# Two transformer blocks on one core: opening by channel halves, two modulation sums moved behind the heads, block two's projection thirds spread over more heads

## Chip, cores and metric

The kernel runs on one core of a Trainium2 chip. The metric is the device time of one execution in microseconds (us), from the first instruction to the last. PE is TensorE, DVE is VectorE, ACT is ScalarE, POOL is GpSimd and SP is SyncE, which issues the loads. PSUM is the accumulator memory of eight banks, SBUF the working memory.

## What is computed

The reference runs two blocks on x (256 tokens x 1024 channels, fp32), one after the other. The part that matters here:

```python
def first_block(x, c, ...):
    mod = c @ w_ada + b_ada                        # 1 x 3072
    shift, scl, gate = jnp.split(mod, 3, axis=-1)
    h = rms_norm(x, g_norm) * (1.0 + scl) + shift
    proj = h @ w_in                                # 256 x 5120
    ...                                            # pooling, 8 heads of attention, two up-projections
    x = x + gate * (merged @ w_out)
    return rms_norm(x, g_final)

def second_block(x, c, ...):
    mod = jax.nn.silu(c) @ w_ada + b_ada           # 1 x 6144
    sh1, sc1, ga1, sh2, sc2, ga2 = jnp.split(mod, 6, axis=-1)
    h = _modulate(_rms_norm(x, g_norm_mix), sh1, sc1)
    proj = h @ w_in
    ...                                            # retention (4 heads) and sparse attention (8 heads)
    x = x + ga1 * (jnp.concatenate([ret_out, nsa_out], -1) @ w_out)
    h = _modulate(_rms_norm(x, g_norm_ffn), sh2, sc2)
    x = x + ga2 * _peer(h, ...)                    # computed densely here, over all 16384 experts
    return _rms_norm(x, g_norm_final)
```

The modulation vectors (shift, scale, gate) are matrix-vector products with large fp32 matrices: `ada1` is that of block one (parts 0 to 5 of 512 columns: 0, 1 shift, 2, 3 scale, 4, 5 gate), `ada2` that of block two (parts 0 to 11).

## The kernel before

**Loads.** The weights of both blocks stream through four slots of 2 MB in SBUF (tile `G`), in the order of the list `STREAM` (l. 63). One entry is a *panel*: 512 output columns for all 1024 input channels, loaded as two halves of 512 channels (1 MB each) by SP (l. 673 to 692). Panel n waits until panel n-4 has been used (`panel_used`, l. 582). Between the panels SP issues x, the constants, the rope tables (`tab`) and the gates.

**The order of everything else** is one list that all engines walk, written out by hand in `steps()` (l. 104): each engine executes its own part of each step, in that order. PSUM banks are handed out from that list: banks 0 to 3 in turn (`turn % 4`, l. 246), 4 and 5 for some fixed uses.

**A projection panel** is computed from two *units* (half a panel each). fp32 operands are split into a rounded "high" and a rest "low"; a unit is three *thirds*, each of 8 matmuls of 128x512: high x high (L1134), high weights x low (L1140), low weights x high (L1146). The weights' high part is made by ACT (`unit_high`, L814), their low part by POOL (L740, four operations of 128x512 per unit). The high part of the activations is made by ACT (L799), the low one by DVE (L1821).

**A modulation sum** (`ada`, `sum_step`, l. 1660 to 1684) is 8 steps on DVE, one for each 128 channels: the first a multiplication (L1677), the rest multiply-add (L1679). The running sum lies either in SBUF (`tab`) or in a PSUM bank (`banks`). PE then adds over the partitions. For one part (the "row" panel) PE makes the product itself instead: `make_row` (L1094), 8 matmuls with one output row, then ACT copies that row and `row_columns` (L1101) turns it into columns. `start_columns` (L1108) adds the partitions of an opening sum; DVE turns the columns into scale and shift (L1776 to 1778, L1788, L1790).

**The opening** computes all four of block one's shift and scale parts (ada1-2, -3 and -1 by DVE, ada1-0 by the row), transposes the normed x (L1072), applies scale and shift while it empties the banks (`turn_out`, L1749 on DVE, L852 on ACT), splits the result, and starts with the products of panel in1-2. `keep_busy` (L1086) issues matmuls whose result nobody reads.

**Block one** goes on with panels in1-2 to in1-9, the last seven of them inside the loop over the 8 attention heads (`heads()`: a step `score` L1295, its softmax on ACT and DVE with L1738 as last, transposition `pT` L1303, product `pv` L1322). Then come `y` (L1932), the units of `poolup` and `attnup`, emptied on DVE (L1948; L1950 with L1952), and `out1`.

**Block two** has its own call of `heads()` for heads 8 to 23, with a table `later` of what PE does after each score: units 35 to 38 whole and units 39, 40 and 41 in thirds, retention (`ret` L1456, `retO` L1466, emptied by L1925), gates (`gate` L2030, over the sums of a head's results), and DVE's pieces of the sums ada2-4 and ada2-5. After the last head come `o`, `mT` (L1072 again) and the output projection (L1161, L1165, L1174). The experts' phase follows; the change does not touch it.

## Time and profile before

| | us |
|---|---|
| median of 3 runs | 1250.8 (1247.75 to 1253.36) |
| profiled execution, its own time | 1252.92 |
| its span in the profile | 1251.1 |
| PE busy | 1198.7 (96%) |
| DVE busy | 902.1 (72%) |
| ACT busy | 619.6 (50%) |
| POOL busy | 552.5 (44%) |
| mean granted clock of PE | 0.986 |

The span is that of one profiled execution; its own time is 1.8 us above the span, and 2.1 us above the median. Timeline rows group neighbouring instructions of one line: start, duration of the group from first start to last end, engine, line, operation, output and inputs, shapes, count, and in brackets the idle time before it with what ended it. In all rows L is a line of the kernel before. PE's fp32 matmuls appear as two records each.

### The profile page before, as it was taken

How to read it: one execution, taken by the hardware profiler on the slowest of the kernel's cores; microseconds unless marked ns; L12 is line 12 of the kernel's file. 1: busy time of each engine (PE TensorE's matmuls, PEld its weight loads, DVE VectorE, ACT ScalarE, POOL GpSimd, SP SyncE). 2: the span in 40 equal slices, each digit the busy share in tenths (PEclk: the TensorE clock that was granted, in tenths of full speed). 3: DMA queues.
4: the chain of work that ended last, by engine and by line, in shares of the span. 5: the costliest groups of instructions: out<-in, count | busy, mean ns of one | idle time of the engine just before them, and what ended most of it. 6: DMA issues, size and time to landing. Idle time of an engine off the chain costs nothing.

```text
span 1251.1 us, 19151 instructions
## 1 busy us (share of the span) xinstructions
PE 1198.7 (96%) x7212; PEld 1049.5 (84%) x7212; DVE 902.1 (72%) x1847; ACT 619.6 (50%) x1079; POOL 552.5 (44%) x323
## 2 busy tenths in 40 slices
PE   4999998999999999999999999999999999999996
PEld 2778877776777899999999999999888888888885
DVE  5678648787667625999768999999556656656666
ACT  1555444454535435444466666555454544545453
POOL 0878759584533005888877777776200000000000
PEclk9999999999988999999999999999999999999998
DMA  9988664353341533656555545555566667666664
GB/s 376 418 337 331 269 269 171 135 208 144 126 152 68 202 135 102 186 183 182 180 165 154 164 156 158 160 155 153 167 223 232 189 220 232 190 190 193 194 193 150
DMA packets 54523, 244.28 MB, mean 195 GB/s; under 512 B 6944, under 2 KB 7328, under 8 KB 42016
## 3 DMA queue, kind: packets, MB, share of 16 engines
q1 hardware_dynamic: 54000, 242.34, 56.6%
q8 instruction: 58, 0.95, 0.3%
q10 hardware_dynamic: 432, 0.72, 0.2%
q14 instruction: 33, 0.27, 0.1%
HBM read 240.94 MB, written 2.10 MB: 194 GB/s over the span
## 4 chain that ended last, share of the span: by engine, by line
PE 88%; DVE 5%; POOL 3%; issue 1%; ACT 1%; DMA 1%; SPq 0%; POOLq 0%; DVEq 0%; ACTq 0%
PE bank L1540 10%; PE bank L1537 10%; PE bank L1536 10%; PE banks L1576 5%; PE bank L1582 5%; PE bank L1576 5%; PE banks L1579 5%; PE banks L1582 5%; PE bank L1579 5%; POOL wq_low_r L740 3%; PE banks L1550 3%; PE banks L1134 2%; PE banks L1140 2%; PE banks L1146 2%; PE bank L1134 2%; PE bank L1140 2%
## 5 line engine op out<-in xcount | busy, mean ns | idle before, releaser
L765 POOL TENSOR_TENSOR split_r<-ring,split_r 128x1024 fp32r<-128x1024 f32 x128 | 307.9, 2406 | 157.3 <-ACT split_r L1000 157.2
L1000 ACT ACTIVATE split_r<-ring 128x1024 fp32r<-128x1024 f32 x256 | 269.2, 1052 | 180.2 <-PE bank L1540 180.2
L1536 PE MATMUL bank<-h_high_r,split_r 128*128 128x256 f32 x1024 | 251.2, 283 | 1.7 <-ACT split_r L1000 1.7
L1537 PE MATMUL bank<-h_low_r,split_r 128*128 128x256 f32 x1024 | 251.1, 283 | 0.0
L2161 DVE TENSOR_TENSOR split_r<-ring,split_r 128x1024 fp32r<-128x1024 f32 x128 | 156.8, 1225 | 65.6 <-ACT split_r L1000 65.6
L1536 PEld LDWEIGHTS bank<-h_high_r,split_r 128*128 128x128 f32 x1024 | 195.8, 191 | 1.9 <-issue 1.9
L1537 PEld LDWEIGHTS bank<-h_low_r,split_r 128*128 128x128 f32 x1024 | 195.9, 191 | 0.0
L769 POOL TENSOR_TENSOR small<-small 128x1 f32<-128x1 f32 x2 | 1.5, 761 | 359.0 <-DVE small L2187 359.0
L740 POOL TENSOR_TENSOR wq_low_r<-G,G_r 128x512 fp32r<-128x512 f32 (+1 forms) x104 | 135.7, 1340 | 49.3 <-ACT G_r L814 49.3
L1540 PE MATMUL bank<-h_high_r,split_r 128*128 128x256 f32 x1024 | 143.7, 283 | 0.2 <-POOL split_r L765 0.2
L1054 ACT ACTIVATE gs_r<-G 128x256 fp32r<-128x256 f32 x128 | 53.5, 418 | 172.5 <-PE bank L1582 172.5
L1540 PEld LDWEIGHTS bank<-h_high_r,split_r 128*128 128x128 f32 x1024 | 132.0, 192 | 0.4 <-POOL split_r L765 0.4
L2109 DVE SCALAR_TENSOR_TENSOR hot_r<-bank,x,w_both_r 128x256 fp32r<-128x256 f32 x256 | 105.5, 472 | 0.0
L2159 DVE TENSOR_TENSOR gs_r<-G,gs_r 128x256 fp32r<-128x256 f32 x128 | 54.3, 424 | 61.8 <-ACT gs_r L1054 61.4
L740 POOL TENSOR_TENSOR wq_low_r<-G,hT_r 128x512 fp32r<-128x512 f32 x48 | 64.4, 1376 | 63.0 <-ACT hT_r L814 63.0
L1576 PE MATMUL banks<-split_r,gs_r 128*128 128x512 f32 x254 | 79.1, 393 | 1.8 <-ACT split_r L1000 1.8
L1582 PE MATMUL bank<-split_r,gs_r 128*128 128x512 f32 x254 | 78.2, 389 | 0.0
L1579 PE MATMUL banks<-split_r,gs_r 128*128 128x512 f32 x254 | 78.2, 389 | 0.0
L1576 PE MATMUL bank<-split_r,gs_r 128*128 128x512 f32 x254 | 78.2, 389 | 0.0
L1579 PE MATMUL bank<-split_r,gs_r 128*128 128x512 f32 x254 | 78.2, 389 | 0.0
L1582 PE MATMUL banks<-split_r,gs_r 128*128 128x512 f32 x254 | 78.2, 389 | 0.0
L814 ACT ACTIVATE G_r<-G 128x2048 fp32r<-128x2048 f32 (+1 forms) x26 | 48.6, 1881 | 21.2 <-DMA G<-in_in 17.9
(455 smaller groups left out, 2247.1 us busy)
## 6 DMA issues: line engine op xcount, KB each, us to landing
ring<-in_down SPq DMA_DIRECT2D x128, 512.0 KB, 3.5
ring<-in_up SPq DMA_DIRECT2D x128, 512.0 KB, 3.5
G<-in_ada SPq DMA_DIRECT2D x32, 1024.0 KB, 10.1
G<-in_in SPq DMA_DIRECT2D x32, 1024.0 KB, 7.2
G<-in_out SPq DMA_DIRECT2D x8, 1024.0 KB, 8.1
G<-in_wq SPq DMA_DIRECT2D x8, 1024.0 KB, 7.7
tab<-in_ada SPq DMA_DIRECT2D x4, 1024.0 KB, 5.8
G<-in_poolup SPq DMA_DIRECT2D x2, 1024.0 KB, 6.3
```

Source lines behind the costliest of these rows:

```text
L740: pool.tensor_tensor(low[:, c, :], raw_half[:, c, :], high[:, c, :].bitcast(F32), ALU.subtract)\
L765: pool.tensor_tensor(wsplit[:, j % SPLIT, 1, :], raw[:, j % RAW, :], wsplit[:, j % SPLIT, 0, :].bitcast(F32), ALU.subtract).then_inc(low_r ...
L1000: nc.scalar.activation(wsplit[:, n % SPLIT, 0, :], raw[:, n % RAW, :], ACT.Copy).then_inc(high_ready, 1)
L1536: mm(o, w[0][:, c, :], h_high[:, c, :], start=(c == 0), stop=False)
L1537: mm(o, w[0][:, c, :], h_low[:, c, :], start=False, stop=False)
L1540: ins = mm(o, w[1][:, c, :], h_high[:, c, :], start=False, stop=(c == C - 1))
L1576: mm(o, g[0][:, tok], w[:, 0, cols], start=(n == 0), stop=False, skip_group_check=True)
L1579: mm(o, g[1][:, tok], w[:, 0, cols], start=False, stop=False, skip_group_check=True)
L1582: ins = mm(o, g[0][:, tok], w[:, 1, cols], start=False, stop=False, skip_group_check=True)
L2109: ins = stt(out=O2[m % 2][:, t, :, :], in0=iota_p.unsqueeze(1).to_broadcast([P, 2, P]), scalar=picks[:, 1, tok:tok + 1], in1=w_both[:, :, ...
L2159: tt(gs[n % 2][1], Gv[:, n, :], gs[n % 2][0].bitcast(F32), ALU.subtract).then_inc(gs_low, 1)
L2161: tt(wsplit[:, n % SPLIT, 1, :], raw[:, n % RAW, :], wsplit[:, n % SPLIT, 0, :].bitcast(F32), ALU.subtract)\
```

## The change

**Opening.** The order of the load queue is now written out (`LOADS`), and the opening works by halves of the channels. The first half's scale (ada1-2) and shift (ada1-0, now a DVE sum) come first; the row panel is now ada1-3 (the second half's scale); ada1-1 (the second half's shift) is loaded after the first halves of in1-2 and in1-3 and summed with its running sum in PSUM. The four keep_busy matmuls of the opening are dropped. PE begins the products of both panels' first halves before the second half of the activations exists. From in1-4 on a projection panel is loaded ahead of the modulation panel it is paired with, and each modulation sum stands one panel later; the gates are loaded later, on a semaphore of their own.

**Behind block one's heads.** The sum of ada2-6 (before: inside the heads) and that of ada2-7 (before: 4 + 4 steps behind `y`, running sum in SBUF) now both stand behind `y`, 8 + 8 steps, running sums in PSUM.

**Block two.** Thirds of units 39 to 41 are spread over more heads, three `busy` steps (two unread matmuls each) are put in, the gates stand one head later, and pieces of the sums ada2-4 and ada2-5 move.

```diff
+STREAM += [("ada1", 2, PANEL, "dve"), ("ada1", 0, PANEL, "dve"), ("ada1", 3, PANEL, "row"), ("in1", 2, PANEL, "pe"),
+           ("in1", 3, PANEL, "pe"), ("ada1", 1, PANEL, "dve")]
+for a, b in ((("in1", 4), ("ada1", 4)), (("in1", 5), ("ada1", 5)), (("in1", 0), ("ada2", 2)), ...
+LOADS = [(0, 0), (0, 1), (1, 0), (1, 1), (2, 0), (2, 1), (3, 0), (4, 0), (5, 0), (5, 1), (3, 1), (4, 1)]
+LOADS += [(n, half) for n in range(6, len(STREAM)) for half in range(2)]
...
-    high("in1", 2, (0,))
-    out.extend(("xT", 0, t, half) for t in range(NT) for half in range(2))
-    high("in1", 2, (1,))
-    panel("in1", 2)
+    out.extend([("high", 0), ("xT", 0, 0, 0), ("xT", 0, 1, 0), ("xsplit", 0), ("row",), ("high", 1), ("high", 2), ("high", 3),
+                ("mods",), ("xT", 0, 0, 1), ("xT", 0, 1, 1), ("xsplit", 1), ("proj", "in1", 2, 0), ("proj", "in1", 2, 1)])
...
     out.append(("y",))
-    last = AT["ada2", 7]
-    for n in ada_after(AT[("poolup", None)], ada):
+    last = (AT["ada2", 6], AT["ada2", 7])
+    for n in ada_after(last[0], ada):
         out.append(("ada", n))
-    out.extend(("sum", last, c) for c in range(4))
+    out.extend(("sum", last[0], c) for c in range(C))
     out.append(("high", 23))
     out.extend(("up", "poolup", t, 1) for t in range(NT))
     out.extend(("oT", t) for t in range(NT))
-    out.extend(("sum", last, c) for c in range(4, C))
+    ...
+    out.extend(("sum", last[1], c) for c in range(C))
...
-        [("high", 41), ("third", 39, 0), ("ret", 0), ("ret", 1), ("third", 39, 1), ("third", 39, 2), ("high", 42)] + both(2),
-        [("retO", 0), ("retO", 1), ("ret", 2), ("ret", 3)] + piece(0, 5, 7),
-        [("retO", 2), ("retO", 3), ("retC",), ("high", 43), ("gate_load",)] + piece(0, 7, 8),
-        [("third", 40, 0), ("third", 40, 1), ("gn",)],
-        [("third", 40, 2), ("rn", 0), ("rn", 1)],
-        [("third", 41, 0), ("third", 41, 1), ("ada", gate[0])] + piece(1, 0, 2),
+        [("high", 41), ("third", 39, 0), ("ret", 0), ("ret", 1), ("third", 39, 1), ("high", 42)] + piece(0, 7, 8),
+        [("third", 39, 2)] + both(2),
+        [("retO", 0), ("retO", 1), ("ret", 2), ("ret", 3), ("busy", 0)],
+        [("retO", 2), ("retO", 3), ("retC",), ("high", 43), ("gate_load",)],
+        [("gn",), ("third", 40, 1), ("third", 40, 2)],
+        [("rn", 0), ("rn", 1), ("third", 41, 0)],
+        [("third", 41, 1), ("ada", gate[0])] + piece(1, 0, 2),
         [("third", 41, 2)] + piece(1, 2, 4),
-        [("gate", 0)] + piece(1, 4, 5),
-        [("gate", 1), ("mT", 1, 0, 0)] + piece(1, 5, 6),
-        [("mT", 1, 1, 0), ("wout_head", 0), ("high", 44)] + piece(1, 6, 8)],
+        [("gate", 0)],
+        [("gate", 1), ("mT", 1, 0, 0)],
+        [("mT", 1, 1, 0), ("wout_head", 0), ("high", 44)]],
...
-         8: [("cmpT", 0), ("cmpT", 1)], 9: [("cmpO", 0), ("cmpO", 1)], 12: both(3)}, 2)
+         8: [("cmpT", 0), ("cmpT", 1)], 9: [("cmpO", 0), ("cmpO", 1), ("third", 40, 0)], 13: both(3),
+         14: [("busy", 1)], 15: [("busy", 2)]}, 2)
+    out.extend(piece(1, 4, 8))
...
-                part = ps[4 + k % 2][:, :] if START <= k < BLOCK_ONE else a
+                part = ps[7][:, :] if k == START - 1 else ps[4 + k % 2][:, :] if START <= k < BLOCK_ONE else a
```

On PE in the opening, from its first row. Before (L1108 `start_columns`, L1072 transposes, L1094 the row, L1134/L1140/L1146 a unit's thirds):

```order
L1108 MATMUL banks<-keep,tab 128x1 x4
L1072 MATMUL bank<-keep,G 128x128 x8
L1072 MATMUL banks<-keep,G 128x128 x8
L1108 MATMUL banks<-keep,tab 128x1 x4
L1094 MATMUL bank<-G,small 1x512 x8
L1086 MATMUL bank<-keep 128x384
L1101 MATMUL bank<-keep,G 128x1 x4
L1108 MATMUL bank<-keep,tab 128x1 x4
L1086 MATMUL banks<-keep 128x384 x3
L1134 MATMUL bank<-hT_0_r,ring_r 128x512 x8
```

Now (the same operations, at lines 1119, 1083, 1104, 1112 and 1143 to 1155 of the changed kernel):

```order
L1119 MATMUL banks<-keep,tab 128x1 x4
L1083 MATMUL bank<-keep,G 128x128 x8
L1083 MATMUL banks<-keep,G 128x128 x8
L1104 MATMUL bank<-G,small 1x512 x4
L1119 MATMUL banks<-keep,tab 128x1 x4
L1104 MATMUL bank<-G,small 1x512 x4
L1143 MATMUL banks<-hT_0_r,ring_r 128x512 x8
L1149 MATMUL banks<-hT_0_r,G_r 128x512 x8
L1155 MATMUL banks<-wq_low_r,ring_r 128x512 x8
L1112 MATMUL bank<-keep,G 128x1 x4
L1119 MATMUL bank<-keep,tab 128x1 x4
L1143 MATMUL bank<-G_r,ring_r 128x512 x8
```

The first unit's three thirds now stand ahead of the row's columns and of the third `start_columns`.

On DVE behind block one's heads, from `y` to the emptying of attnup. Before:

```order
L1932 TENSOR_TENSOR G<-bank,G 128x512 x2
L1706 TENSOR_TENSOR small<-bank,small 128x4
L1677 TENSOR_SCALAR tab<-G,small 128x512
L1679 SCALAR_TENSOR_TENSOR tab<-G,small,tab 128x512 x3
L1948 SCALAR_TENSOR_TENSOR G<-G,bank 128x512
L1948 SCALAR_TENSOR_TENSOR G<-G,banks 128x512
L1992 TENSOR_TENSOR G_r<-banks,ring_r 128x4x128
L1992 TENSOR_TENSOR G_r<-bank,ring_r 128x4x128
L1679 SCALAR_TENSOR_TENSOR tab<-G,small,tab 128x512 x4
L1950 SCALAR_TENSOR_TENSOR G<-G,bank 128x512
```

Now:

```order
L1968 TENSOR_TENSOR G<-bank,G 128x512 x2
L1737 TENSOR_TENSOR small<-bank,small 128x4
L1740 TENSOR_SCALAR small<-small 128x4
L1741 TENSOR_TENSOR small<-small 128x4
L1703 TENSOR_SCALAR banks<-G,small 128x512
L1705 SCALAR_TENSOR_TENSOR banks<-G,small,banks 128x512 x6
L1705 SCALAR_TENSOR_TENSOR tab<-G,small,banks 128x512
L1984 SCALAR_TENSOR_TENSOR G<-G,banks 128x512 x2
L2028 TENSOR_TENSOR G_r<-bank,ring_r 128x4x128 x2
L1734 TENSOR_TENSOR small<-banks,small 128x4
L1703 TENSOR_SCALAR banks<-G,small 128x512
L1705 SCALAR_TENSOR_TENSOR banks<-G,small,banks 128x512 x6
```

Two whole sums stand there in place of one, and their running sum is in `banks` (PSUM), not in `tab` (SBUF).

On PE in block two, from score 22 on (L1295/L1296 score, L1072 `mT`, L1303 pT, L1322 to L1324 pv, L1161 the output projection). Before:

```order
L1295 MATMUL banks<-G 128x128
L1296 MATMUL banks<-G 128x256
L1072 MATMUL banks<-keep,ring 128x128 x4
L1303 MATMUL bank<-keep,rows 128x128 x3
L1322 MATMUL bank<-G,ring 128x64
L1323 MATMUL bank<-G,ring 128x64
L1324 MATMUL bank<-G,ring 128x64
L1295 MATMUL bank<-G 128x128
L1296 MATMUL bank<-G 128x256
L1072 MATMUL banks<-keep,ring 128x128 x4
L1161 MATMUL banks<-G_r,ring_r 128x512 x4
```

Now (L1321/L1322 score, L1329 pT, L1348 to L1350 pv, L1097 a busy step, L1083 `mT`):

```order
L1321 MATMUL bank<-G 128x128
L1322 MATMUL bank<-G 128x256
L1329 MATMUL banks<-keep,rows 128x128 x3
L1348 MATMUL bank<-G,ring 128x64
L1349 MATMUL bank<-G,ring 128x64
L1350 MATMUL bank<-G,ring 128x64
L1097 MATMUL banks<-keep 128x384 x2
L1321 MATMUL bank<-G 128x128
L1322 MATMUL bank<-G 128x256
L1083 MATMUL bank<-keep,ring 128x128 x4
L1329 MATMUL banks<-keep,ring 128x128 x3
```

The first `mT` (which needs gate 0) now stands behind score 23, where it stood behind score 22, and a busy step stands ahead of score 23.

## Rows read from the trace of the kernel before

**Rows 1.** The page: busy times, granted clock in 40 slices, the chain that ended last

```profile
PE 1198.7 (96%) x7212; PEld 1049.5 (84%) x7212; DVE 902.1 (72%) x1847; ACT 619.6 (50%) x1079; POOL 552.5 (44%) x323
...
PEclk9999999999988999999999999999999999999998
...
PE 88%; DVE 5%; POOL 3%; issue 1%; ACT 1%; DMA 1%; SPq 0%; POOLq 0%; DVEq 0%; ACTq 0%
```

**Rows 2.** PE's waits over the whole span: total us, times, longest us

```profile
PE banks L1108 <- DMA small<-in_cb: 13.3, 1, 13.3
...
PE banks L1072 <- DVE ring L2030: 2.7, 2, 1.7
...
PE bank L1134 <- DVE G L1948: 1.8, 1, 1.8
...
PE banks L1295 <- DVE ring L1925: 1.3, 1, 1.3
```

**Rows 3.** PE's timeline, 0 to 75 us: start us, us, then the group

```profile
21.94 8.72 PE L1094 MATMUL bank<-G,small 128*1 128x512 f32 x16
...
36.56 2.06 PE L1134 MATMUL bank<-hT_r,ring_r 128*128 128x512 f32 x8 [1.05 <-DVE G L1749]
...
58.94 1.39 PE L1134 MATMUL bank<-G_r,ring_r 128*128 128x512 f32 x5 [0.17 <-issue]
...
69.94 1.02 PE L1205 MATMUL banks<-tab,keep 128*128 128x512 f32 x2
...
71.80 1.12 PE L1072 MATMUL bank<-keep,G 128*128 128x128 f32 x8 [0.40 <-ACT G L878]
...
73.38 0.63 PE L1072 MATMUL banks<-keep,G 128*128 128x128 f32 x4 [0.47 <-DVE rows L1700]
...
74.79 0.46 PE L1295 MATMUL banks<-G 64*128 64x128 f32 x2 [0.78 <-ACT G L901]
```

**Rows 4.** DVE's timeline, 0 to 80 us

```profile
14.91 0.49 DVE L1677 TENSOR_SCALAR tab<-G,small 128x512 f32<-128x512 f32 x1 [2.56 <-DMA G<-in_ada]
15.43 5.47 DVE L1679 SCALAR_TENSOR_TENSOR tab<-G,small,tab 128x512 f32<-128x512 f32 x7
...
24.96 0.48 DVE L1677 TENSOR_SCALAR tab<-G,small 128x512 f32<-128x512 f32 x1 [2.27 <-DMA G<-in_ada]
...
50.06 0.76 DVE L1677 TENSOR_SCALAR banks<-G,small 128x512 f32<-128x512 f32 x1
50.85 4.71 DVE L1679 SCALAR_TENSOR_TENSOR banks<-G,small,banks 128x512 f32<-128x512 f32 x6
```

**Rows 5.** ACT's timeline, 0 to 80 us

```profile
31.30 1.89 ACT L814 ACTIVATE hT_r<-G 128x2048 fp32r<-128x2048 f32 x1
...
33.83 1.51 ACT L852 ACTIVATE G<-banks,small 128x128 f32<-128x128 f32 x4 [0.64 <-DVEq L1791]
```

**Rows 6.** POOL's timeline, 0 to 80 us

```profile
33.27 5.96 POOL L740 TENSOR_TENSOR wq_low_r<-G,hT_r 128x512 fp32r<-128x512 f32 x4 [18.62 <-ACT hT_r L814]
```

**Rows 7.** DVE's timeline, 185 to 196 us

```profile
188.07 1.29 DVE L1932 TENSOR_TENSOR G<-bank,G 128x512 f32<-128x512 f32 x2 [1.17 <-PE bank L1324]
...
190.55 5.06 DVE L1679 SCALAR_TENSOR_TENSOR tab<-G,small,tab 128x512 f32<-128x512 f32 x3
```

**Rows 8.** Windows: stretch, busy us of each engine, PEclk, DMA share, GB/s

```profile
349.00:361.00 12.00, 12.00 (x46) 9.61 (x45) 8.89 (x36) 5.33 (x14) 2.00 (x2) 0.57 0.60 201
383.00:391.00 8.00, 6.98 (x26) 5.46 (x25) 7.40 (x21) 3.64 (x12) 0.00 (x0) 0.57 0.06 26
```

**Rows 9.** PE's timeline, 354 to 421 us

```profile
354.34 3.78 PE L1134 MATMUL banks<-hT_r,ring_r 128*128 128x512 f32 x8
...
364.39 2.12 PE L1146 MATMUL banks<-wq_low_r,ring_r 128*128 128x512 f32 x8
...
417.22 4.03 PE L1086 MATMUL bank<-keep 128*128 128x384 f32 x12
```

**Rows 10.** SP's queue: its timeline, 130 to 215 us

```profile
173.10 22.12 SPq L679 DMA_DIRECT2D G<-in_out  x4
```

More of the change, by code:

```diff
@@ L844, in _ @@
                     ins.then_inc(ready, 1)
+                elif kind == "row":
+                    act.wait_ge(row_full, 1)
+                    nc.scalar.activation(row, ps[6][0:1, :], ACT.Copy).then_inc(row_copied, 1)
+                elif kind == "xsplit":
+                    for q in range(NT):
+                        x0_high_part(q, s[1])
                 elif kind == "xT" and s[2] == 1:
@@ L855, in _ @@
                     bank_free(ins, s)
-                    for q in range(NT):
-                        x0_high_part(q, half)
                 elif kind == "high":
@@ L1113, in _ @@
             start_columns(0)
-            opening = [s for s in STEPS if s[0:2] == ("xT", 0)]
-            for _, _, t, half in opening:
-                if half == 0:
+            opening = [s for s in STEPS if s[0:2] == ("xT", 0) or s[0:2] == ("proj", "in1") and s[2] in (2, 3)]
+            for half in range(2):
+                for t in range(NT):
                     pe_.wait_ge(xn_ready, t + 1)
-                transposes(("xT", 0, t, half), [xn[0][:, t, (4 * half + c) * P:(4 * half + c + 1) * P] for c in range(4)])
+                    transposes(("xT", 0, t, half), [xn[0][:, t, (4 * half + c) * P:(4 * half + c + 1) * P] for c in range(4)])
+            make_row(0)
             start_columns(1)
-            make_row()
-            keep_busy(ps[7], 1)
-            row_columns()
-            start_columns(2)
-            keep_busy(ps[4], 3)
+            make_row(1)
             def products(k, outs, x_high, x_low, chunk, x_ready, thirds=(0, 1, 2)):
@@ L1191, in m_ready, with in1_products, x_ready @@
                 return wait
+            def in1_products(i, halves, fill):
+                steps_ = [("proj", "in1", i, t) for t in range(NT)]
+                outs = [(bank_to_fill(pe_, step) if fill else ps[USE[step][0]], slice(t * P, (t + 1) * P), step)
+                        for t, step in enumerate(steps_)]
+                for half in halves:
+                    def x_ready(low):
+                        pe_.wait_ge(x0_low_ready if low else x0_high_ready, 1 + half if low else 2 + 2 * half)
+                    products(UNIT[AT["in1", i], half], [(o[:, :], tok, step) for o, tok, step in outs],
+                             x0_high, x0_low, 4 * half, x_ready)
+            in1_products(2, (0,), True)
+            row_columns()
+            start_columns(2)
+            in1_products(3, (0,), True)
+            in1_products(2, (1,), False)
+            in1_products(3, (1,), False)
             for s in STEPS:
@@ L1209, in _ @@
                     bank_full(ins, s)
+                elif kind == "busy":
+                    bank = bank_to_fill(pe_, s)
+                    keep_busy(bank, 1).then_inc(full[USE[s][0]], 1)
+                    keep_busy(bank, 1).then_inc(freed[USE[s][0]], 1)
                 elif kind == "warm":
@@ L1697, in ada_out @@
                     g = gateA if name == "ada1" else gate2
+                    if name == "ada1" and half == 0:
+                        dve.wait_ge(gates_in, 48)
                     if name == "ada2" and half == 0:
```

139 lines of the change are left out of this document (71 added, 68 removed).

## Prediction

> **What bounds the kernel now.** I read the page first: PE is busy for 1198.7 of 1251.1 us, and the chain that ended last is 88% PE [rows 1]. So a microsecond is won only where PE stands still, runs slowly, or has matmuls taken away. Next the granted clock by slices: 9 nearly everywhere, with two 8s in the slices from 344 to 407 us and one in the last slice [rows 1]. Then PE's waits, longest first [rows 2]: 13.3 us at the start for the first constants, and behind it only waits of 1 to 3 us. Last the timelines of the two places that the change touches: the opening, where real products start at 36.56 us [rows 3], and block two's heads, where PE has light work and runs at 1.2 instead of 2.4 GHz in two stretches [rows 8]. The experts' phase, two thirds of the span, is not touched.
>
> A measurement of this kernel can tell about 0.5% from no change, 6.25 us of 1250.8.
>
> **The opening.** The load queue sets its pace. The sum of ada1-3 starts at 14.91 and that of ada1-1 at 24.96, each when its first half lands, four halves apart [rows 4]: 2.51 us a half. In the new order, counted from ada1-0's first half at 14.9 (the same place in the queue): ada1-3 at 19.9 and 22.4, in1-2's first half at 25.0, in1-3's at 27.5, ada1-1 at 30.0 and 32.5, the two second halves at 35.0 and 37.5, then the tables and in1-4.
>
> The first product needs unit 0's weights and half 0's activations. ACT rounds the weights in 1.89 us [rows 5], 25.0 to 26.9. It then empties half 0's banks, 1.51 us [rows 5], and rounds the result group by group behind that; I put the activations at 29.4. The shift is in time: ada1-0's sum takes 0.49 + 5.47 us [rows 4] and ends at 20.9. PE meanwhile makes the row, 8.72 us in all [rows 3]: the first half from 19.9 to 24.3, start_columns, the second half until about 29. The first product starts at **29.7** instead of 36.56.
>
> From there four units take 22.4 us, as in the rows (36.56 to 58.94 [rows 3]). Between the first and the second now stand the row's columns and the third start_columns, 1.9 us together. The latter waits for the sum of ada1-1, which starts at about 31.1, when DVE has split half 0, and takes 0.76 + 4.71 + 0.8 = 6.3 us in PSUM [rows 4]: 37.4. PE is there at 36.2, a **new wait of 1.2**. 29.7 + 22.4 + 1.9 + 1.2 = 55.2: in1-4 starts 3.7 us before its 58.94.
>
> Between in1-4 (11.0 us, until 69.94) and score 0 stand three waits of 0.40, 0.47 and 0.78 us [rows 3]. The second is on the gate row of ada1-4, whose product moves a panel later; the other two are on ACT's copies of in1-4, which now start with fewer roundings ahead of them. I take 1.4 of the 1.65. The moved product (1.02 us [rows 3]) comes back inside the heads and counts as no gain. The four keep_busy matmuls that go stood under a wait for DVE: nothing. The opening: **-5.1**. If DVE's sum were no wait at all it would be -6.3; if half of the head start were eaten by landings and splits, -1.7.
>
> The sum's price rests on where its running sum lies. While POOL works, a step takes 1.69 us with it in SBUF (5.06 us for 3 [rows 7]) and 0.785 in PSUM (4.71 for 6 [rows 4]). The Trainium skill, "SBUF — State Buffer", section "SBUF: two separate sides", gives a rule for this: a DVE operation with two SBUF inputs and a GpSimd operation lock one port pair against each other. By that rule, the trace agrees. A rule against the change stands in "VectorE: DVE Perf Modes" of the Trainium skill, section "Why PSUM operands drop a tier": an operand in PSUM rules out the mode that uses both read ports. Here the first step takes 0.76 us in PSUM against 0.49 in SBUF, the next ones 0.785 against 5.47 / 7 = 0.78 [rows 4]. If all eight steps of the two moved sums paid this 0.27, each sum would lose 2.2 us instead of 0.27, and the total below would be 3.8 smaller; by the rows only the first step pays, and that is inside the 6.3.
>
> **Behind block one's heads** PE waits for DVE (1.8 us at L1134 [rows 2]). From `y` (188.07 [rows 7]) on, DVE had one sum in SBUF, 0.8 + 7 x 1.69 = 12.6 us; it now has two in PSUM, 2 x 6.3 = 12.6. Three more small operations come with the sums: **+0.5**. That ada2-6's sum leaves the heads gains nothing, since DVE has slack there. Its slot comes free later, about 196 instead of 170. SP's queue shows out1's loads issued over 22.12 us from 173.10 [rows 10]; the first of them now waits until 196. Load, rounding and POOL's four operations (5.96 at most [rows 6]) take about 13 us more: 209, where PE comes to that unit no earlier than 209 to 214. Hidden, with little to spare.
>
> **Block two.** Removed: the wait of 1.3 us for L1925 and the two for L2030, 2.7 [rows 2], because a third, busy matmuls or another head now stand ahead. The window 349 to 361 has a granted clock of 0.57, so 12 x 0.43 = 5.2 us are lost in it; 383 to 391 likewise 8 x 0.43 = 3.4 [rows 8]. At half clock a third takes 3.78 us instead of 2.12 [rows 9]. Before the first fall PE had some 10 us of the heads' and retention's small matmuls with a wait among them; one third (39, 2) and one busy step now stand there. Before the second it had the waits for the gates; a third and two busy steps now stand there. I take both as mended. Added: three busy steps of two matmuls. Twelve records, six matmuls, take 4.03 us [rows 9], so six cost **+4.0**. New waits: the gates and `o` follow closer behind norm and DVE's moved pieces. No row shows them; between none and twice those that they replace (5.4) I take 2.7, the size of the two at L2030. Sum: -1.3 - 2.7 - 5.2 - 3.4 + 4.0 + 2.7 = **-5.9**.
>
> **Together** -5.1 + 0.5 - 5.9 = -10.5. The profiled execution, 1252.9 us by its own time (span 1251.1 and 1.8 around it), becomes 1242.4. It lies 2.1 above the median, so the median becomes 1250.8 - 10.5 = **1240.3**.
>
> **Rivals.**
>
> 1. *The clock falls all the same* in one light stretch of block two or in both, perhaps shifted. For it: two matmuls of 0.67 us are little in a stretch of 10 us of small ones. Against it: where thirds stand between the heads (361 to 383) the clock stayed up. It gives back 5.2, 3.4 or 8.6: 1245.5, 1243.7 or 1248.9. The Trainium skill, "TensorE: Matmul & The Clock Gate", Part 1, calls the chip's look at activity free-running, not tied to the program; by that, the same order could fall in one run and not in another. Chance 0.16 for one stretch, 0.06 for both.
>
> 2. *The opening is limited elsewhere.* ACT now has three roundings (3 x 1.89) between the two halves of the activations, and the sum of ada1-1 runs beside POOL. If the sum went at 1.69 us a step it would take 6.3 us longer and eat the gain: 1246.6. If landings and ACT eat half the head start (3.4), 1243.7. Chance 0.15.
>
> 3. *Slower: block two's thirds no longer hold the clock.* They are now single, with a head between each. If PE stays at 1.2 GHz from the first third on, nothing is mended (+8.6), and 14 us of work that ran at full clock between 361 and 383 takes twice as long (+14): 1240.3 + 22.6 = 1262.9. It decides once the clock's loss is 16.8 us above the forecast's, half clock over some 34 us in a row. Against it: the total of dense matmuls there is unchanged and six more are added. Chance 0.04.
>
> 4. *out1's first unit is late*, because its slot waits for ada2-6's sum: PE waits up to 5 us, 1245. Chance 0.04.
>
> **How the numbers follow.** Forecast 0.55, with its own range 1236.4 to 1243.5 (new waits none or twice, the opening's wait). The predicted time is its 1240.3. The range 1235.8 to 1247.3 takes in the forecast, one stretch at half clock, the limited opening and the late unit; what is outside, both stretches, rival 3 and a remainder, is under 0.2. Faster by over 0.5% means under 1244.5: the forecast, half of rival 1's single stretch, half of rival 2, and a little of the rest, 0.73. Within: 0.21. Slower, over 1257: rival 3 and unknowns, 0.06.
>
> **What would show it.** In the profile after: the first product at 29.7, the third start_columns waiting 1 us or so for L1705, in1-4 at 55.2 (right within 1.5); score 0 near 69; behind `y` two groups of six L1705 at 4.7 us each; the slices of block two with a granted clock of 9 throughout; no wait for the ret emptying. Wrong: a window of block two at 0.5, L1705 steps over 1 us, a wait for the rounding of out1's first unit, or from the last head to the experts no shift kept.

## Result and the profile after

The changed kernel is a little slower. Beside the kernel before, on the same chips, its median is 1254.9 us (20 runs) against 1250.8 (20 runs): ratio 1.0032, interval 1.002 to 1.0045. Two more comparisons, made with the experiments, give 1.0024 (1.0006 to 1.0043) and 1.0027 (1.0014 to 1.004). By the bound of 0.5% that is no change; against the forecast of 1240.3 it is a loss of 3 to 4 us where a gain of 10.5 was expected, and it lies outside the range.

The profiled execution took 1252.81 us, its span is 1251.0, so it equals that of before (1252.92, 1251.1) and lies 2 us below its own median. The two traces therefore show where the forecast gain of 10.5 went, and the experiments have to show the 4 us between the medians.

The page: busy times and the granted clock ([rows 1] before).

```profile
PE 1199.7 (96%) x7216; PEld 1050.2 (84%) x7216; DVE 908.9 (73%) x1847; ACT 620.3 (50%) x1079; POOL 551.0 (44%) x323
...
PEclk9999998999998999999999999999999999999999
```

The clock row has an 8 at 188 to 219 us now, which is new, and one at 375 to 407; the one at 344 to 375 is gone.

PE's waits (total, times, longest); in [rows 2] the same wait for the emptying of poolup is 1.8 us and that of `start_columns` on the third sum did not exist.

```profile
PE banks L1237 <- DVE G L1984: 3.6, 1, 3.6
...
PE bank L1119 <- DVE tab L1705: 0.7, 1, 0.7
```

PE's timeline in the opening, beside [rows 3].

```profile
29.29 2.08 PE L1143 MATMUL banks<-hT_r,ring_r 128*128 128x512 f32 x8 [1.33 <-ACT ring_r L807]
...
36.66 1.05 PE L1119 MATMUL bank<-keep,tab 128*128 128x1 f32 x8 [0.68 <-DVE tab L1705]
...
55.63 2.08 PE L1143 MATMUL banks<-G_r,ring_r 128*128 128x512 f32 x8 [1.09 <-issue]
...
69.53 0.46 PE L1321 MATMUL bank<-G 64*128 64x128 f32 x2 [0.99 <-ACT G L912]
```

The opening did what was forecast: first product at 29.29 (29.7 foretold), the third `start_columns` 0.68 us late (1.2), in1-4 at 55.63 (55.2) instead of 58.94, score 0 at 69.53 (near 69) instead of 74.79. The 55.63 holds a little luck: PE started 0.4 us early and waited 0.5 less than foretold, and then stood 1.09 us ahead of in1-4, which nobody had forecast and for which the profile shows no releaser. 5.3 us are won there. They are still there at `y`: 182.76 against 188.07 [rows 7].

Then they are gone. PE's timeline behind `y`; L1170 is the first product of the output projection in the changed kernel; it is L1161 in the kernel before, whose row stands by itself below:

```profile
193.53 1.82 PE L1237 MATMUL banks<-keep,tab 128*128 128x1 f32 x8 [3.59 <-DVE G L1984]
195.21 2.05 PE L1143 MATMUL banks<-G_r,ring_r 128*128 128x512 f32 x4
...
214.00 1.19 PE L1170 MATMUL bank<-hT_r,G_r 128*128 128x512 f32 x4 [0.98 <-DVE ring_r L2035]
```

```profile
213.36 1.19 PE L1161 MATMUL banks<-hT_r,G_r 128*128 128x512 f32 x4 [0.61 <-DVE ring_r L1999]
```

DVE's timeline, same stretch:

```profile
182.76 1.29 DVE L1968 TENSOR_TENSOR G<-bank,G 128x512 f32<-128x512 f32 x2 [1.17 <-PE bank L1350]
184.19 0.16 DVE L1737 TENSOR_TENSOR small<-bank,small 128x4 f32<-128x4 f32 x1
184.39 0.93 DVE L1740 TENSOR_SCALAR small<-small 128x4 f32<-128x4 f32 x1
185.35 1.20 DVE L1741 TENSOR_TENSOR small<-small 128x4 f32<-128x4 f32 x1
186.59 0.76 DVE L1703 TENSOR_SCALAR banks<-G,small 128x512 f32<-128x512 f32 x1
187.38 4.71 DVE L1705 SCALAR_TENSOR_TENSOR banks<-G,small,banks 128x512 f32<-128x512 f32 x6
...
192.80 1.28 DVE L1984 SCALAR_TENSOR_TENSOR G<-G,banks 128x512 f32<-128x512 f32 x2
```

The last one is the emptying of poolup's banks. The same operation in the kernel before, where `y` starts at 188.07 [rows 7]:

```profile
195.65 0.69 DVE L1948 SCALAR_TENSOR_TENSOR G<-G,bank 128x512 f32<-128x512 f32 x1
```

POOL's timeline in the changed kernel:

```profile
181.51 5.03 POOL L750 TENSOR_TENSOR wq_low_r<-G,G_r 128x512 fp32r<-128x512 f32 x4
```

From `y` to the output projection it is 31.2 us (182.76 to 214.00), before 25.3 (188.07 to 213.36). The reader sees three things: two operations of 128x4 that take 0.93 and 1.20 us while POOL works, where their neighbour takes 0.16; behind them a whole sum, before DVE can empty poolup's banks, for which PE waits 3.59 us; and behind that wait products at half speed.

The rows price each. DVE reaches the emptying 10.0 us after `y` (182.76 to 192.80) and before 7.6 (188.07 to 195.65). The two small operations take 2.2 of the 2.5 us more (184.39 to 186.59). The whole sum takes hardly more than the half sum did, 6.2 against 6.0, because a step beside POOL costs 0.785 us in PSUM and 1.69 in SBUF. On PE the 5.9 us are 1.8 of longer wait, 0.95 for the product of ada2-6, which had stood inside the heads, and 3.2 of lost clock.

Windows: stretch, busy us per engine, PEclk, DMA share, GB/s.

```profile
156.00:160.00 4.00, 4.00 (x12) 2.78 (x12) 2.57 (x8) 0.99 (x4) 0.00 (x0) 0.57 1.02 428
194.00:201.00 7.00, 7.00 (x22) 5.76 (x22) 6.64 (x11) 2.52 (x2) 1.10 (x1) 0.54 0.97 384
349.00:361.00 12.00, 11.71 (x64) 8.72 (x63) 5.46 (x19) 6.17 (x15) 0.00 (x0) 1.00 0.23 82
377.00:389.00 12.00, 11.36 (x36) 7.64 (x37) 9.81 (x26) 6.36 (x20) 0.00 (x0) 0.57 0.36 152
```

194 to 201 lost 7 x 0.46 = 3.2 us of clock. In block two the stretch 349 to 361 has the full clock (0.57 before [rows 8]), but 377 to 389 has 0.57, a loss of 5.2 where before 3.4 were lost at 383 to 391. PE's timeline there:

```profile
377.64 0.67 PE L1329 MATMUL banks<-keep,rows 128*128 128x128 f32 x3 [1.22 <-DVE rows L1768]
...
379.60 2.87 PE L1097 MATMUL banks<-keep 128*128 128x384 f32 x4
...
386.69 2.24 PE L1097 MATMUL banks<-keep 128*128 128x384 f32 x4
```

The second busy step itself takes 2.87 us, and 1.51 where the clock holds (see the trace of tail_undone below). From the third (39, 0) to the first `mT` of the second half it is 64.7 us (332.91 to 397.64) against 65.4 before (332.84 to 398.22): block two gives 0.7 us where 5.9 were forecast.

### The profile page after: what moved, and what is told of

The parts are those of the page before. It is cut to its first block, busy times and chain, and to the rows that moved or that the text cites. A ratio compares the mean times of both kernels' runs of the same rounds, so it can differ in the third digit from the quotient of the medians.

```text
span 1251.0 us, 19166 instructions
## 1 busy us (share of the span) xinstructions
PE 1199.7 (96%) x7216; PEld 1050.2 (84%) x7216; DVE 908.9 (73%) x1847; ACT 620.3 (50%) x1079; POOL 551.0 (44%) x323
## 4 chain that ended last, share of the span: by engine, by line
PE 88%; DVE 5%; POOL 2%; ACT 2%; issue 2%; DMA 1%; SPq 1%; POOLq 0%; DVEq 0%; ACTq 0%
PE bank L1566 10%; PE bank L1563 10%; PE bank L1562 10%; PE banks L1602 5%; PE bank L1602 5%; PE banks L1608 5%; PE bank L1608 5%; PE banks L1605 5%; PE bank L1605 5%; PE banks L1143 3%; PE banks L1149 3%; PE banks L1155 3%; PE banks L1576 3%; POOL wq_low_r L750 2%; PE bank L1143 1%
## 6 DMA issues: line engine op xcount, KB each, us to landing
G<-in_ada SPq DMA_DIRECT2D x32, 1024.0 KB, 10.2
```

## The experiments

All times are medians; a ratio is to the kernel before on the same chip and in the same rounds. "Below the changed kernel" compares with its 1254.55 of after_again, for the runs from early_out to gap_again on another chip; the kernel before took 1252.2 to 1252.7 on these chips, so such a difference is good to half a microsecond at best. The traces of the new opening reach score 0 at 69.5 to 71.2 us, those of the old one at 74.4 to 75.2.

### Which part costs what

The changed kernel again:

> The changed kernel again, unaltered, for a second trace. Theory A (the part behind block one's heads gives the opening's gain back, in every execution alike): the median within 1.5 us of 1254.9, score 0 near 69.5 us, and from y's start to the first mT product of the output projection 31.2 us again, against 25.3 in the kernel before. Theory B (what the first trace shows is chance, and other executions lose elsewhere, in loads that land late or in the clock): that stretch differs by more than 1.5 us from 31.2, or a stretch elsewhere is several us longer than in the first trace.

Measured: 1254.55 (12 runs), ratio 1.0024 (1.0006 to 1.0043). From `y` to the output projection 31.7 us, so that loss is no chance. But score 0 to `y` took 115.3 us instead of 113.2, so both theories have a piece of the truth. The three following take a part back.

```diff
 # blocktwo_undone: the table of heads() of block two, its small steps and piece(1, 4, 8) as before
-        [("high", 41), ("third", 39, 0), ("ret", 0), ("ret", 1), ("third", 39, 1), ("high", 42)] + piece(0, 7, 8),
-        [("third", 39, 2)] + both(2),
+        [("high", 41), ("third", 39, 0), ("ret", 0), ("ret", 1), ("third", 39, 1), ("third", 39, 2), ("high", 42)] + both(2),
...
 # tail_undone: ada2-6 inside the heads, ada2-7 4 + 4 steps in SBUF, as before
-    last = (AT["ada2", 6], AT["ada2", 7])
+    last = AT["ada2", 7]
...
-                    ahead = [a for a in ada_steps[:-4] if a[1] < AT[(s[1], s[2])] + 3]
+                    ahead = [a for a in ada_steps[:-3] if a[1] < AT[(s[1], s[2])] + 3]
 # opening_only: both edits
```

> The change without its part in block two (thirds, pieces, gates as before, no busy steps). Theory A: in the first trace that part is worth 0.65 us, so within 1.5 us of the changed kernel, 1255.5. Rival C (block two's light stretches lose the clock at other places from run to run, and the busy steps then cost without gain): 3 to 4 us faster than the changed kernel, 1251.

Measured: 1255.28, ratio 1.0032 (1.0016 to 1.0047), 0.7 above the changed kernel. That agrees with the 0.7 us of the trace, though the medians alone do not separate it from nothing. Rival C falls.

> The change with the sums behind block one's heads as before: ada2-6 inside the heads, ada2-7 in 4 + 4 steps with the running sum in SBUF; opening and block two as changed. Theory A: the stretch from y to the first product of the output projection shrinks from 31.2 to about 26 to 27 (the small operations on DVE stay late), so 4 to 5 us faster than the changed kernel, 1250. Theory B: no faster than it, 1255.

Measured: 1252.62, ratio 1.002 (0.9996 to 1.0044), so the part behind the heads costs about 1.9 us, not 4 to 5. In its trace `y` to the output projection is still 29.6 us, where theory A had 26 to 27.

> The opening and the new order of loads alone; the sums behind the heads and block two as before. Theory A: the 5.3 us won at score 0 survive less 1, so 1246.5, faster than before by 0.35%. Theory B: the gain of the opening shows in one trace and not in the median, 1250 to 1255.

Measured: 1252.86, ratio 1.0018 (0.9997 to 1.0038): the opening alone gains nothing, though score 0 comes at 70.85. A miss for theory A's 1246.5; the median is the one that theory B foretold. Its trace has 30.8 us behind `y`, with the sums of before: the order of the sums is not what costs most there. DVE's and PE's timelines:

```profile
186.06 0.88 DVE L1735 TENSOR_SCALAR small<-small 128x4 f32<-128x4 f32 x1
186.97 1.20 DVE L1736 TENSOR_TENSOR small<-small 128x4 f32<-128x4 f32 x1
```

```profile
196.16 2.04 PE L1138 MATMUL banks<-G_r,ring_r 128*128 128x512 f32 x4 [3.66 <-DVE G L1979]
```

These are ada2-9's scale, which in the kernel before is worked out inside the heads at 173.25, as POOL ended: 0.17 and 0.16 us. The new order of loads (in1 ahead of ada) moved its product behind `y`, whatever is done with ada2-6. With half a sum ahead of the emptying, as before, PE waits 3.66 us (1.8 before) and loses 3.4 us of clock behind it.

### Behind the heads

```diff
 # early_out: ada2-9's product ahead of poolup's first half
+              [("adas", AT["ada2", 9] + 1), ("high", 22), ("up", "poolup", 0, 0), ("up", "poolup", 1, 0)]]
 # before_psum: the kernel before with one line changed
-                    sum_step(n, k, c, acc[k % 2], acc[k % 2])
+                    sum_step(n, k, c, ps[4 + k % 2][:, :] if k < BLOCK_ONE else acc[k % 2], acc[k % 2])
 # tail_split: opening_only with both of these
```

(`adas` issues the pending products of the modulation sums, as `panel` does.)

> The changed kernel with one step moved: the product of ada2-9 and its two small operations on DVE (L1740, L1741, 0.93 and 1.20 us beside POOL behind y, in the changed kernel's trace) stand ahead of poolup's first half instead of behind y. Theory A (these small operations and that product hold back the sum, and with it attnup): the wait of PE for the emptying of poolup falls from 3.6 to about 1, the half-clock stretch behind it goes, y to the first product of the output projection 31.2 to about 27, median 1251. Theory B (the sum of ada2-6 ahead of the emptying is what holds PE back, 6.3 us by itself): wait still 1.5 to 2.5, clock still lost, median 1253 or more.

Measured: 1253.93, ratio 1.002 (1.0007 to 1.0033). The wait for the emptying fell from 3.6 to 2.15 us, and 1.7 instead of 3.4 us of clock were lost behind it (197 to 201). Each theory has a part: wait and median lie where theory B put them, but `y` to the output projection is 27.7 us, near theory A's 27. The median cannot decide here, because in the trace score 0 to `y` took 116.8 us, 3.4 of that more lost clock than in the first trace.

> The kernel before with one line changed: ada2-7's running sum in PSUM. The price of a step beside POOL falls from 1.69 to 0.785, so the wait of 1.8 us at attnup goes and attnup's end comes 1.8 earlier; the later waits of 1.0 and 0.6 go or stay. Theory A: 2 us faster than the kernel before. If DVE is not what bounds that stretch: no difference.

Measured: 1250.53 against 1252.16, ratio 0.9985 (0.9973 to 0.9997). PE's timeline, from the first product of attnup to the output projection:

```profile
194.00 1.17 PE L1134 MATMUL bank<-G_r,ring_r 128*128 128x512 f32 x4 [0.83 <-ACT ring_r L930]
...
210.35 1.19 PE L1161 MATMUL banks<-hT_r,G_r 128*128 128x512 f32 x4 [1.44 <-DVE ring_r L1999]
```

The wait for DVE is gone (what stays is 0.83 for ACT) and `y` to the projection is 24.4 us instead of 25.3. One line, 1.6 us in the median, 0.9 of them in this stretch.

> Opening as changed, block two as before; behind the heads a third way: ada2-6 inside the heads, ada2-9's product ahead of poolup, ada2-7 in 4 + 4 steps but with its running sum in PSUM (3.1 us each four instead of 5.9). Theory A: the wait for the emptying of poolup goes (under 0.5 us), no half clock there, y to the output projection 24 to 25 us, and the opening's 4 to 5 us come through: 1246 to 1247. Theory B (the opening's gain is lost for another reason in most executions): 1251 or more.

Measured: 1249.68, 2.5 below before, though the ratio, 0.9995 (0.9978 to 1.0011), does not separate them, and 3 above theory A's figure. 24.3 us behind `y`, as expected; but score 0 to `y` took 116.8. 4.9 us are won against the changed kernel, and only 0.9 against before_psum on the same chip, which is within the noise: the new opening, worth 3.4 us at score 0 in these two traces, is worth 1 or nothing at the end.

Then the sums went where DVE is idle:

```diff
 # gap
-              [("high", 22), ("up", "poolup", 0, 0), ("up", "poolup", 1, 0)]]
+              [("adas", AT["ada2", 9] + 1), ("high", 22)] + [("sum", AT["ada2", 6], c) for c in range(6)] +
+              [("up", "poolup", 0, 0), ("up", "poolup", 1, 0)]]
...
     out.append(("y",))
...
+    out.extend(("sum", last[0], c) for c in (6, 7))
+    out.extend(("sum", last[1], c) for c in range(2))
     out.append(("high", 23))
     out.extend(("up", "poolup", t, 1) for t in range(NT))
     out.extend(("oT", t) for t in range(NT))
...
+    out.extend(("sum", last[1], c) for c in range(2, C))
+    out.extend([("high", 24), ("high", 25)])
+    out.extend(("up", "attnup", t, 0) for t in range(NT))
+    for n in ada_after(AT["ada2", 6] + 1, ada):
...
```

> The changed kernel with DVE's sums spread into its idle time at the end of the heads: six steps of ada2-6 while PE makes poolup's first half (DVE idles 4.3 us there in the changed kernel), two behind y with two of ada2-7, and ada2-7's other six beside attnup's products; ada2-9's product ahead of poolup, ada2-6's between attnup's halves. Theory A (DVE's order behind the heads eats the opening's gain): no wait for L1984 over 1 us, y to the output projection 24 to 25 us instead of 31.2, 5 to 6 us faster than the changed kernel, 1249. Theory B (the gain is lost by slower executions of another cause): within 2 us of the changed kernel.

Measured: 1250.27, ratio 0.9991 (0.9973 to 1.0008), 4.3 below the changed kernel. DVE's timeline (L1743, L1744 ada2-9's scale, L1706, L1708 the sum, L1971 `y`):

```profile
177.28 0.17 DVE L1743 TENSOR_SCALAR small<-small 128x4 f32<-128x4 f32 x1
177.48 0.16 DVE L1744 TENSOR_TENSOR small<-small 128x4 f32<-128x4 f32 x1
177.68 0.76 DVE L1706 TENSOR_SCALAR banks<-G,small 128x512 f32<-128x512 f32 x1
178.47 3.92 DVE L1708 SCALAR_TENSOR_TENSOR banks<-G,small,banks 128x512 f32<-128x512 f32 x5
...
184.90 1.29 DVE L1971 TENSOR_TENSOR G<-bank,G 128x512 f32<-128x512 f32 x2 [1.17 <-PE bank L1353]
```

PE's timeline:

```profile
192.02 2.09 PE L1146 MATMUL banks<-G_r,ring_r 128*128 128x512 f32 x8 [0.83 <-ACT ring_r L944]
...
209.31 1.19 PE L1173 MATMUL bank<-hT_r,G_r 128*128 128x512 f32 x4 [1.20 <-DVE ring_r L2038]
```

The small operations take 0.17 and 0.16 again, the six steps fit before `y`, attnup's first product waits 0.83 us and not 3.6, and `y` to the projection is 24.4 us.

> The kernel before, opening and block two untouched, with the same spreading of ada2-6 and ada2-7 at the end of the heads. Theory A: y to the output projection 24 us or less instead of 25.3, 1250 or a little below, against 1251 to 1252 of before; the difference to the version with the new opening is what the opening is really worth, 3 to 5 us by the traces. If the opening is worth nothing in the median, the two are equal.

Measured: 1251.44, ratio 0.9996 (0.9984 to 1.0008). The same 24.4 us behind `y`. The new opening with block two's part, gap against before_gap, is worth 1.2 us here, and 3.6 and 2.5 by gap's two later medians (gap_again and gap_third, on other chips), where 3 to 5 were expected.

### Block two

```diff
 # gap_one_busy: the two late busy steps out; no_busy: the first one, ("busy", 0), as well
-         8: [("cmpT", 0), ("cmpT", 1)], 9: [("cmpO", 0), ("cmpO", 1), ("third", 40, 0)], 13: both(3),
-         14: [("busy", 1)], 15: [("busy", 2)]}, 2)
+         8: [("cmpT", 0), ("cmpT", 1)], 9: [("cmpO", 0), ("cmpO", 1), ("third", 40, 0)], 13: both(3)}, 2)
```

> The changed kernel without the three busy steps. If they hold the clock up: the first stretch of block two (around 350 us) falls to half clock and gives 3 to 5 us back for 1.3 saved, and the time rises to 1257. If only the spread thirds hold it there and the two late busy steps run at half clock themselves (2.9 and 2.2 us in the trace) in place of waits: 1 to 2.5 us faster, 1252.5.

Measured: 1256.61 (9 runs), ratio 1.0063 (1.0039 to 1.0086), 2 us above the changed kernel and 2.7 above early_out on the same chip. But in its trace the first stretch keeps the clock, so the thirds alone can hold it; the clock falls at 383 to 393 (5.1 us). That it fell there is no proof that the busy steps hold the second stretch: with them the first and the third trace of the changed kernel lost the same 5.1 us. What speaks for them are the medians, here and in gap_one_busy below. So the expectation's 1257 came, but not for the reason that it gave, a fall in the first stretch.

> The same, and ada2-8's product no longer stacked on ada2-1's behind in1-8 (in all traces of the new opening the clock fell behind those two, 4 us of small matmuls, at 156 us, 1.7 us lost; not in the kernel before). If the stack causes the fall: full clock from 150 to 165 and 1.7 us faster than the version with the stack. Otherwise the same.

```diff
-        sums = ada_after(AT[(name, i)] + (2 if (name, i) == ("in1", 8) else 0), ada)
+        sums = ada_after(AT[(name, i)], ada)
```

Measured: 1250.06 against 1250.27 of gap. The clock at 156 us stayed up, and fell at 175 to 182 instead, behind a wait of 3.0 us. No gain. The expectation is wrong in its premise: of the 15 traces that have the new opening and the two products together, 11 fall at 156 to 158 us, and after_again, changed_third and tail_split keep the clock there and fall at 176 to 178. So one trace does not show that taking the products apart did it.

> The last version with the first busy step alone; the two late ones, which themselves ran at half clock in the changed kernel's trace, are left out. All three gone cost 2 us. If the first one does that work: this is 0 to 2 us faster than with all three. If the late ones do it: 2 us slower.

Measured: 1252.59, ratio 1.0014 (0.9998 to 1.0029), 2.5 above gap_one_product (0.9999, 0.9978 to 1.002): by the medians the late busy steps do the work, though the two traces lose the same 5.1 us of clock in block two. In a trace where the clock held, PE's timeline (tail_undone) shows what block two then is:

```profile
379.94 0.55 PE L1327 MATMUL banks<-keep,rows 128*128 128x128 f32 x3 [1.21 <-DVE rows L1766]
...
381.28 1.51 PE L1095 MATMUL banks<-keep 128*128 128x384 f32 x4
...
384.93 0.66 PE L1081 MATMUL bank<-keep,ring 128*128 128x128 f32 x4 [1.29 <-DVE ring L2064]
...
386.36 1.51 PE L1095 MATMUL banks<-keep 128*128 128x384 f32 x4
389.49 0.66 PE L1081 MATMUL bank<-keep,ring 128*128 128x128 f32 x4 [1.62 <-DVE ring L2064]
```

The busy steps take 1.51 us in place of 2.87, and the waits for norm and the gates come back: 1.21 + 1.29 + 1.62 = 4.1 us, as much as the 1.3 + 2.7 that were to go [rows 2].

### Where the rest of the opening's gain goes

In 6 of the first 11 traces with the new opening, score 0 to `y` is 2 to 3.6 us longer than 113.3. In five of them PE waits 1.5 to 3.0 us for head 7's softmax (1.1 to 1.4 otherwise), while POOL makes the low part of poolup beside it; in the sixth only the clock fell. The wait itself is thus 0.4 to 1.9 us longer; in all but after_again another 1.7 to 3.4 us are clock that the first trace did not lose. The load order was changed, and with it one line that keeps every engine's order the same:

```diff
-STREAM += [("ada2", 6, PANEL, "dve"), ("poolup", None, PANEL, "pe"), ("attnup", None, PANEL, "pe"), ("ada2", 7, PANEL, "dve"),
+STREAM += [("poolup", None, PANEL, "pe"), ("ada2", 6, PANEL, "dve"), ("attnup", None, PANEL, "pe"), ("ada2", 7, PANEL, "dve"),
...
-    for n in ada_after(AT["poolup", None], ada):
+    for n in ada_after(AT["attnup", None], ada):
```

> The changed kernel with poolup's panel loaded ahead of ada2-6's, every engine's order the same, SP's alone different. Collision theory: poolup lands some 5 us earlier, POOL's four operations for it end before 170 us instead of at 172.6 to 174.2, and head 7's softmax on DVE (171 to 174) always meets an idle POOL; PE's wait at its pT is 1.2 us or less and score 0 to y 113.3 us in the trace, and the median is 1 to 2 us below the changed kernel's 1254.5. Rival (chance of the clock alone): median within 0.7 us of the changed kernel.

Measured: 1250.69, ratio 0.9988 (0.9973 to 1.0003), 3.9 below the changed kernel's 1254.55; more than the 1 to 2 that were expected. In the trace the wait is 1.13 us and score 0 to `y` 113.4, as foretold.

> The spread sums (six steps of ada2-6 beside poolup's first half, and so on) with poolup's panel loaded first. Both collisions with POOL gone. Collision theory: y by 183 to 184.5, output projection by 207 to 209, median 1247.5 to 1248.5. Rival: as the spread sums without this, 1250.

Measured: 1251.05, ratio 0.9987 (0.9973 to 1.0001). `y` at 183.7 and the projection at 208.1, as expected, but the median misses the expected 1247.5 to 1248.5, and it is 3.2 us above its control in the same rounds, gap_again below (0.8 above gap, on another chip). In its trace PE waits 2.6 us for POOL at 219 us, behind the output projection's start. So the exchange helps the changed kernel and, by these medians, not this one, although the collision is gone in both.

> The spread sums again, unaltered, as the control of the line above and for a second trace. Median within 1 us of its 1250.3. Collision theory: where the wait for L1769 is 1.2, score 0 to y is 113 to 114 us; where it is 2.5 to 3, it is 115.4 to 117 and the clock falls behind it.

Measured: 1247.88 (7 runs), ratio 0.9961 (0.9946 to 0.9976). Both halves of the expectation miss: the median lies 2.4 us below 1250.3, and the wait was 1.34 us with a stretch of 116.3, because the clock had fallen at 158 and 178 without a long wait.

The changed kernel with and without the exchange, on one chip:

> The changed kernel a third time, as the control of the next line on the same chip. Collision theory: median near 1254.5, 2 us or so above before. Rival (the two differ by the chip or the hour): near the next line.

> The changed kernel with poolup's panel loaded first, again, beside its control. Collision theory: 2.5 to 4 us below the line above, POOL's poolup operations over before 170 us. Rival: less than 1 us apart.

Measured: **1255.85 and 1250.81**, 5.0 us apart where 2.5 to 4 were expected; ratios to before 1.0027 (1.0014 to 1.004) and 1.0 (0.9975 to 1.0025). The two intervals overlap: 3 of the 12 runs with the exchange took 1258.9 to 1260.3 us. DVE's, POOL's and PE's timelines of changed_third:

```profile
173.79 0.73 DVE L1755 TENSOR_SCALAR small<-small 128x2 f32<-128x2 f32 x1
...
174.62 1.44 DVE L1766 TENSOR_SCALAR ring<-ring,small 128x128 f32<-128x128 f32 x2
```

```profile
170.77 4.95 POOL L750 TENSOR_TENSOR wq_low_r<-G,ring_r 128x512 fp32r<-128x512 f32 x4 [12.94 <-ACT ring_r L822]
```

```profile
176.12 0.55 PE L1329 MATMUL bank<-keep,ring 128*128 128x128 f32 x3 [2.58 <-DVE ring L1766]
```

and of pool_first_again:

```profile
175.58 0.17 DVE L1755 TENSOR_SCALAR small<-small 128x2 f32<-128x2 f32 x1
...
175.84 0.55 DVE L1766 TENSOR_SCALAR ring<-ring,small 128x128 f32<-128x128 f32 x2
```

```profile
164.45 5.04 POOL L750 TENSOR_TENSOR wq_low_r<-G,ring_r 128x512 fp32r<-128x512 f32 x4 [8.01 <-ACT ring_r L822]
```

```profile
176.45 0.55 PE L1329 MATMUL bank<-keep,ring 128*128 128x128 f32 x3 [1.12 <-DVE ring L1766]
```

With POOL busy until 175.7, L1755 takes 0.73 us and the pair L1766 1.44, and PE waits 2.58. With POOL done at 169.5 they take 0.17 and 0.55, and PE waits 1.12. The order on PE, DVE, ACT and POOL is the same in both. So the collision is real and costs 1.5 us at this place. It is not shown to be the whole 5.0: the output projection starts 2.5 us earlier (215.8 against 218.3), and 1.8 of these are won between `y` and it (29.9 us against 31.7), where both traces with the exchange lose 1.7 us of clock and all three of the changed kernel 3.4. Why the order of loads changes that, no run shows.

> The spread sums a third time, as the candidate for a version that beats both kernels: 1248 to 1250, 2 to 4 us below before and 5 below the changed kernel. If the second result (1247.9 of 7 runs) was chance: 1250.3, and its interval against before takes in 1.

Measured: 1248.94, ratio 0.9978 (0.9956 to 1.0). Over its three comparisons (31 runs) this version is below the kernel before each time, by 1.9, 4.7 and 3.8 us in the medians; only the second interval stays clear of 1. Against the changed kernel beside it, it is 6.9 us faster. It beats the changed kernel, and lies about 0.2% below the kernel before, which two of the three comparisons cannot tell from nothing.

## Why the prediction was wrong

**The opening** was right to 0.5 us at each of its marks. What failed is the step behind it, that its 5.1 us are carried to the end. The first trace carries them to `y`, but after_again and changed_third take 2.1 and 2.3 us longer from score 0 to `y`. The forecast moved PE and DVE and left POOL out: POOL starts on poolup at 167.6 us in the changed trace (169.3 and 170.8 in its other two) and at 168.3 in the one before. That start hangs on a load (the rounding ahead of it is released by poolup's DMA) and has not moved forward, while head 7's softmax comes 4 us earlier and can run into it. Where it does, PE waits up to 1.9 us longer. Taking that collision away by the load order went with 3.9 and 5.0 us in two comparisons of the changed kernel, more than the wait, and with a loss of 0.8 to 3.2 in gap. Rival 2, "the opening is limited elsewhere", did not occur: the loss lies behind the opening, where no rival looked.

**Behind the heads** +0.5 was forecast; the trace has +5.9. The term that failed is the one for "three more small operations", put at nearly nothing without a row; two of them take 2.1 us, because POOL works beside them. The price stood in the trace of the kernel before, in DVE's and POOL's timelines at the heads:

```profile
100.73 0.70 DVE L1712 TENSOR_SCALAR small<-small 128x4 f32<-128x4 f32 x1
101.47 1.20 DVE L1713 TENSOR_TENSOR small<-small 128x4 f32<-128x4 f32 x1
```

```profile
100.14 5.01 POOL L740 TENSOR_TENSOR wq_low_r<-G,G_r 128x512 fp32r<-128x512 f32 x4
```

The sum of 12.6 against 12.6 us was right, and so nearly was the part of it ahead of the emptying of poolup (6.2 us now, 6.0 before). The wait at attnup grew from 1.8 to 3.6 for the most part by the small operations, as opening_only shows with its 3.66. The product of ada2-6 (1.82 us at half clock) stands in PE's way behind that wait, and that a wait of this length is followed by lost clock (3.2 us) was not in the sum at all. Rival 4 did not occur: out1's unit was in time.

**Block two** -5.9 was forecast; 0.7 came, by median and by trace. The three busy steps cost about 4 us as reckoned (1.46 to 1.51 us each where the clock held). Two terms were mis-sized. The new waits are 4.1 us where the clock holds, not 2.7. And the clock was mended in part. Summed over 332 to 399 us, the lost clock is 3.4 to 10.2 us in the six traces with the block two of before (mean 7.1), and 0 to 5.1 in the twelve with the changed one and all its busy steps (mean 2.6): 4.5 us saved and not 8.6. So -4.5 + 4.0 + 4.1 - 4.0 = -0.4, near the 0.7 measured. These are means over different kernels, so the agreement is a rough one. It is rival 1: the clock fell in 8 of those 12 traces, and its chance of 0.22 was too low. Rival 3 did not occur: in the first trace the stretch 349 to 361 kept the full clock.

**The two rules on ports** in the prediction came out like this. What the Trainium skill, "SBUF — State Buffer", section "SBUF: two separate sides", says of the port pair was used for the sums and not applied to the other operations of DVE; by that rule L1741, with two operands in SBUF, has to wait for POOL, and the trace agrees (1.20 us). L1740 and L1755, with one such operand, are slowed as well (0.93 and 0.73); whether they run in the mode with both ports, which the same rule names, no run shows. What the Trainium skill, "VectorE: DVE Perf Modes", section "Why PSUM operands drop a tier", says did not decide: before_psum, which moves a sum to PSUM, is 1.6 us faster.

**Open.** The terms account for the two first traces: 5.3 won, 5.9 lost, 0.7 won, and the spans are equal. That the median lies 4 us higher is explained in part: the other two traces of the changed kernel lose 2 us more between score 0 and `y` and 0.5 more behind it. The exchange of loads gives back 4 to 5 us in the changed kernel, 1.5 of them seen as the collision, and costs 0.8 to 3.2 in gap; what else it does is not known. New opening and old also differ in their tails: 20 of 204 executions with the new one took 1258 us or more, 1 of 199 without it. None of them fell on a profiled execution, so their cause is not shown.

## What to carry to other kernels

Time won early on one engine is kept only if every engine and every load that it will meet later is moved with it; look for the first place where another engine's work is tied to a load and not to the engine that got faster. Small DVE operations in SBUF are not free beside GpSimd: count them at about 1 us each there, or put them where GpSimd rests, and look for one of their kind in the trace at hand before a term is called small. A sum that fills idle time belongs ahead of a wait only as far as the idle time reaches; one step more delays what stands behind it, and lost clock can follow the wait.

## What the runs showed of the hardware

A DVE operation of 128x4 in SBUF took 0.16 to 0.17 us by itself. Beside POOL operations of 128x512 the one with two operands in SBUF took 1.20 (L1741 in the changed kernel, L1713 in the one before) and the TENSOR_SCALAR ahead of it 0.70 to 1.38 (L1712 in the kernel before; L1740 behind `y`: 0.93 in the first trace of the changed kernel, 1.37 and 1.38 in the other two). Its nearest neighbour that reads PSUM (L1737, 0.16) was not slowed.

The clock falls at different places from execution to execution. The changed kernel lost 15.0, 10.0 and 16.3 us to it in its three traces (one less the mean granted clock of 0.988, 0.992 and 0.987, times the span); in block two it ran at half clock from 378 to 388 us in the first and from 381 to 385 in the second. In most traces of the new opening it fell at 156 us, behind two products of 128x1 matmuls in a row and a head's small matmuls, but not in all, as said above. One trace is not enough to price a change that rests on the clock.
